# Scores of layer 0 in pairs, a padded router row, and gate and up products three experts ahead

## The reference

```
layer 0 attention: projection -> 8 attention heads (64 wide, rotary, causal)
                   + 4 retention heads (64 wide keys, 128 wide values, decay,
                     group norm, swish gate) -> output projection
layer 1 attention: projection -> 16 heads, dilated causal windows -> output projection
experts (both):    g = top1(x @ w_group + b_group)          # 4 groups
                   i = top2 of (x @ w_fine + b_fine) in g   # 8 experts a group
                   out[t] += gate * (silu(x @ w_gate[e]) * (x @ w_up[e])) @ w_down[e]
```

## Time and profile before

| | |
|---|---|
| median of 3 runs | 1133.7 us (1133.15 to 1136.21) |
| profiled execution | 1135.6 us, span 1133.7 us |
| TensorE busy | 861.8 us (76% of the span) |
| TensorE weight load busy | 547.3 us (48%) |
| VectorE, ScalarE, GpSimd busy | 383.3, 244.2, 37.8 us |
| DMA | 440.71 MB, mean 389 GB/s |
| mean granted TensorE clock | 0.883 |

### The profile page before, as it was taken

The page is one execution under the profiler, slowest core; times in us unless marked ns, Lnnn a source line. Parts: engine busy times, 40 slices in busy tenths (PEclk is TensorE's granted clock), DMA queues, the critical chain, the costliest instruction groups (busy, mean ns, idle before and its releaser), DMA issues.

```text
span 1133.7 us, 21763 instructions
## 1 busy us (share of the span) xinstructions
PE 861.8 (76%) x9154; PEld 547.3 (48%) x9154; DVE 383.3 (34%) x940; ACT 244.2 (22%) x624; POOL 37.8 (3%) x59
## 2 busy tenths in 40 slices
PE   8999979967675657576899999798566666666774
PEld 6876735534343434243478776455243434343432
DVE  6886523322120212121188763333121212121212
ACT  5565401100000100000165763111000000000012
POOL 0014000000000000000000220000000000000000
PEclk9998989988687878888999999899787879797887
DMA  9967889999999999999996577999999999999995
GB/s 344 277 288 298 366 331 412 430 427 428 431 427 428 430 428 428 429 428 428 415 386 276 213 309 287 419 427 429 428 428 429 427 430 428 427 430 428 428 428 217
DMA packets 54417, 440.71 MB, mean 389 GB/s; under 512 B 11873, under 2 KB 12385, under 8 KB 29538
## 3 DMA queue, kind: packets, MB, share of 16 engines
q1 hardware_dynamic: 54368, 440.07, 93.5%
q10 hardware_dynamic: 2, 0.00, 0.0%
HBM read 439.01 MB, written 1.05 MB: 388 GB/s over the span
## 4 chain that ended last, share of the span: by engine, by line
PE 43%; DMA 40%; SPq 5%; DVE 4%; another core or an unknown queue 3%; ACT 3%; issue 2%; POOL 0%; POOLq 0%; ACTq 0%; DVEq 0%
DMA ring<-in_w_expert_up 30%; PE bank L1039 13%; DMA ring<-in_w_expert_down 9%; PE bank L1060 5%; PE bank L933 3%; PE bank L935 3%; PE bank L934 3%; SPq L449 3%; PE bank L1073 3%; PE bank L1021 2%; PE bank L1121 1%; SPq L453 1%; PE bank L1123 1%; PE bank L1122 1%
## 5 line engine op out<-in xcount | busy, mean ns | idle before, releaser
L1039 PE MATMUL bank<-ring,scratch 128*32 128x256 f32 x4096 | 302.2, 460 | 177.8 <-DMA ring<-in_w_expert_up 176.4
L1039 PEld LDWEIGHTS bank<-ring,scratch 128*32 128x32 f32 x4096 | 156.5, 132 | 319.1 <-issue 208.5
L1488 DVE TENSOR_SCALAR scratch<-scratch 128x128 f32<-128x128 f32 x64 | 14.5, 227 | 634.3 <-ACT scratch L726 612.5
L725 ACT ACTIVATE scratch<-bank 128x128 f32<-128x128 f32 x64 | 17.7, 277 | 587.6 <-PE bank L1039 568.9
L1060 PE MATMUL bank<-ring,h 128*32 128x256 f32 x2048 | 127.2, 390 | 11.3 <-DMA ring<-in_w_expert_down 11.3
L1073 PE MATMUL bank<-h 32*128 32x256 f32 x1024 | 75.5, 407 | 37.2 <-ACT h L733 37.2
L1060 PEld LDWEIGHTS bank<-ring,h 128*32 128x32 f32 x2048 | 63.1, 111 | 55.8 <-issue 24.1
L1073 PEld LDWEIGHTS bank<-h 32*128 32x128 f32 x1024 | 50.9, 188 | 67.1 <-issue 67.0
L933 PE MATMUL bank<-split,h_high 128*128 128x512 f32 x192 | 77.6, 404 | 2.0 <-DVE split L1302 1.4
L934 PE MATMUL bank<-split,h_low 128*128 128x512 f32 x192 | 75.1, 391 | 0.0
L935 PE MATMUL bank<-split,h_high 128*128 128x512 f32 x192 | 75.1, 391 | 0.0
(11 more groups left out here) (166 smaller groups left out, 741.9 us busy)
## 6 DMA issues: line engine op xcount, KB each, us to landing
ring<-in_w_expert_gate SPq DMA_DIRECT2D x64, 2048.0 KB, 47.3
ring<-in_w_expert_up SPq DMA_DIRECT2D x64, 2048.0 KB, 48.8
ring<-in_w_expert_down SPq DMA_DIRECT2D x62, 2048.0 KB, 48.5
ring<-in_w_in_even SPq DMA_DIRECT2D x5, 2048.0 KB, 17.9
ring<-in_w_in_odd SPq DMA_DIRECT2D x5, 2048.0 KB, 20.5
ring<-in_w_out_even SPq DMA_DIRECT2D x2, 2048.0 KB, 8.3
ring<-in_w_expert_down SPq DMA_DIRECT2D x4, 1024.0 KB, 44.4
ring<-in_w_out_odd SPq DMA_DIRECT2D x2, 2048.0 KB, 12.9
```

The costliest lines, as they stand in the source:

```text
L1039: last = pe.matmul(psum[6][32 * j:32 * j + 32, 0:2 * P].rearrange("p (a s) -> p a s", a=2), xT[:, c, SLOTS * k:SLOTS * k + SLOTS], ring[:, ...
```

## The change

- In layer 0 the scores of two heads are issued together, each pair waiting for both maxima of the pair before. VectorE works by pairs too: two maxima, a step of the retention statistics, then the two reciprocals. The four retained products are split, two behind the first pair of scores and two behind the second. The power steps on GpSimd go ahead of head 4 in place of head 3, and the two gating products come after all heads.
- The router's logits become one row of 40 columns: 4 groups, 4 columns of padding (zero weight, bias of -3e38), 32 experts. VectorE makes it in one operation in place of two and masks in place. The filler between the two counting parts is one product of 512 columns and one of 128 in place of two of 512.
- Gate and up products run three experts ahead (`AHEAD` 3 in place of 2). The third product goes behind the start of the sums; SP reloads pairs 4, 5 and 6 before down 4; the gather of the next group comes one expert earlier. In a layer's last group the filler, or the spreading of the gain row, stays behind steps 0 and 1, while the last gate and up product now stands behind step 0.
- Some small tiles move. `SPLIT_FIRST` keeps the old value 2 where the projection of layer 1 used `AHEAD`.

```
+FINE_AT = 8
+ROUTES = FINE_AT + 32
...
-AHEAD = 2
+AHEAD = 3
+SPLIT_FIRST = 2
...
-        w_rt = sb("w_rt", [P, LAYERS, C, GROUPS + EXPERTS])
-        b_rt = sb("b_rt", [P, LAYERS, GROUPS + EXPERTS])
-        small = sb("small", [P, 320])
+        w_rt = sb("w_rt", [P, LAYERS, C, ROUTES])
+        b_rt = sb("b_rt", [P, LAYERS, ROUTES])
...
-        masked = scratch[:, 1536:1600].rearrange("p (t e) -> p t e", t=T)
-        chosen = scratch[:, 1600:1728].rearrange("p (t c e) -> p t c e", t=T, c=2)
-        lf = scratch[:, 1728:1792].rearrange("p (t e) -> p t e", t=T)
+        routes = scratch[:, 1536:1536 + T * ROUTES].rearrange("p (t e) -> p t e", t=T)
+        lg, lf = routes[:, :, 0:FINE_AT], routes[:, :, FINE_AT:ROUTES]
+        chosen = scratch[:, 1664:1792].rearrange("p (t c e) -> p t c e", t=T, c=2)
...
-                for e in range(EXPERTS - 8, EXPERTS - 6):
+                for e in range(EXPERTS - 2 * GE, EXPERTS - GE - AHEAD):
                     step(r * EXPERTS + e, e, e % GE)
 
             def load_across(l, r):
 
-                for k in range(6):
-                    e = r * EXPERTS + k - 6
-                    next_down(l, e, EXPERTS - AHEAD + k if k < AHEAD else k - AHEAD, (k + AHEAD) % GE)
+                for k in range(GE + AHEAD):
+                    e = r * EXPERTS + k - (GE + AHEAD)
+                    next_down(l, e, EXPERTS - AHEAD + k if k < AHEAD else k - AHEAD, (k - AHEAD) % GE)
...
-                for e in range(2):
+                for e in range(AHEAD):
...
-                next_down(l, more * EXPERTS + EXPERTS - 6, EXPERTS - 2, GE - 2)
+                for e in range(EXPERTS - GE - AHEAD, EXPERTS - GE - 1):
+                    next_down(l, more * EXPERTS + e, e + GE, e % GE)
...
-                    if l == 0 and m == 3:
+                    if l == 0 and m == 4:
...
-                    if l == 0 and m >= HEADS[0] - T:
-                        t = m - (HEADS[0] - T)
+                if l == 0:
+                    for t in range(T):
...
-                        parts(AHEAD if l else 1, 4)
+                        parts(SPLIT_FIRST if l else 1, 4)
...
-                    pe.wait_ge(s_out[l], m - 1 if l == 0 else m - 2)
+                    pe.wait_ge(s_out[l], m if l == 0 else m - 2)
                 elif l == 0:
-                    pe.wait_ge(ret_ready, RET - 1 + m)
-                heads = [(score_bank(l, n), slice(HEAD * (n % 2), HEAD * (n % 2) + HEAD))
-                         for n in ((m,) if l == 0 else (m, m + 1))]
+                    pe.wait_ge(ret_ready, RET)
+                heads = [(score_bank(l, n), slice(HEAD * (n % 2), HEAD * (n % 2) + HEAD)) for n in (m, m + 1)]
                 q, k = qT[:, m // 2, :], kT[:, m // 2, :]
                 for bank, rows in heads:
...
-                elif l == 0 or i % 2 == 0:
+                elif i % 2 == 0:
...
+                    if not after and k < 2:
+                        if l == LAYERS - 1:
+                            spread_gains(k)
+                        else:
+                            keep_warm(4, cst[:, 0:512], psum[5])
                     if k < GE - AHEAD:
-                        if not after and l == LAYERS - 1:
-                            spread_gains(k)
-                        elif not after:
-                            keep_warm(4, cst[:, 0:512], psum[5])
                         gate_up(l, r, g, k + AHEAD)
...
-                    last = pe.matmul(psum[4 + t][:, 0:36], hT(t, q)[:, c - 4 * q, :],
+                    last = pe.matmul(psum[4 + t][:, 0:ROUTES], hT(t, q)[:, c - 4 * q, :],
...
-                        for n in range(n_ret[l]):
+                    if l == 0 and m in (1, 3):
+                        for n in (m - 1, m):
...
-                keep_warm(2, cst[:, 0:512], psum[0])
+                keep_warm(1, cst[:, 0:512], psum[0])
+                keep_warm(1, cst[:, 0:128], psum[0])
...
+                for k in range(2, AHEAD):
+                    gate_up(l, 0, 0, k)
...
-                if m in (2, 3):
-                    t = m - 2
+                if m in (2, 4):
+                    t = m // 2 - 1
...
-                elif m in (6, 7):
...
+            def retention_norm(t):
+
+                if t == 0:
+                    dve.wait_ge(ret_pow, 6)
+                    dve.wait_ge(swished, T)
+                for n in range(RET):
+                    at = RET * t + n
+                    last = dve.tensor_scalar(o_ret[:, t, P * n:P * n + P], psum[6 + t][:, P * n:P * n + P],
+                                             rstat[:, t, n, 0:1], rrstd[:, at:at + 1], ALU.subtract, ALU.mult)
+                last.then_inc(ret_scaled, 1)
...
-                for dst, cols in ((lg[:, t, 0:GROUPS], slice(0, GROUPS)), (lf[:, t, :], slice(GROUPS, 36))):
-                    last = dve.scalar_tensor_tensor(out=dst, in0=bank[:, cols], scalar=rstd[:, t:t + 1],
-                                                    in1=bias[:, cols], op0=ALU.mult, op1=ALU.add)
-                link(last)
+                link(dve.scalar_tensor_tensor(out=routes[:, t, :], in0=bank[:, 0:ROUTES], scalar=rstd[:, t:t + 1],
+                                              in1=bias, op0=ALU.mult, op1=ALU.add))
...
+            dve.memset(w_rt[:, :, :, GROUPS:FINE_AT], 0.0)
+            norm_link(dve.memset(b_rt[:, :, GROUPS:FINE_AT], -FAR))
...
-                    if m < HEADS[l]:
+                    if l and m < HEADS[l]:
                         head_max(l, m)
+                    if l == 0 and m < HEADS[l] and m % 2 == 0:
+                        head_max(l, m)
+                        head_max(l, m + 1)
+                        retention_step(m, link)
+                        head_sum(l, m, link)
+                        if m == HEADS[l] - 2:
+                            retention_norm(0)
+                        head_sum(l, m + 1, link)
+                        if m == HEADS[l] - 2:
+                            retention_norm(1)
...
-                    if 0 < m <= HEADS[l]:
+                    if l and 0 < m <= HEADS[l]:
                         head_sum(l, m - 1, link)
-                    if l == 0 and m <= HEADS[l]:
-                        retention_step(m, link)
...
-                for k in range(AHEAD):
+                for k in range(2):
                     hidden(l, k, k, first=(k == 0))
                 dve.wait_ge(gate_steps, GATE_STEPS * (l + 1))
                 for k in range(AHEAD):
                     gate_slots(l, k, k)
+                for k in range(2, AHEAD):
+                    hidden(l, k, k)
```

More of the change, by code:

```diff
@@ L221, in build @@
         gains_rt = sb("gains_rt", [P, LAYERS, C])
[L222 to L224 removed]
+        w_rt = sb("w_rt", [P, LAYERS, C, ROUTES])
+        b_rt = sb("b_rt", [P, LAYERS, ROUTES])
+        small = sb("small", [P, 306])
         idx_u = sb("idx_u", [P, 2 * T, 8], U32)
@@ L313, in build @@
         bnst = small[:, 258:306].rearrange("p (a s) -> p a s", a=2 * RET)
-        expg = small[:, 306:314].rearrange("p (t e) -> p t e", t=T)
+        expg = small[:, 136:144].rearrange("p (t e) -> p t e", t=T)
         sq4 = small[:, 256:264].rearrange("p (t a) -> p t a", t=T)
-        half_exp = small[:, 314:316]
-        cnt = small[:, 316:318]
-        three_halves = small[:, 318:319]
+        half_exp = small[:, 144:146]
+        cnt = small[:, 146:148]
+        three_halves = small[:, 148:149]
         newton = small[:, 258:266]
-        posm = sb("posm", [P, T, 36])
-        gate = sb("gate", [P, T, 36])
+        posm = sb("posm", [P, T, EXPERTS])
+        gate = sb("gate", [P, T, EXPERTS])
         asg = sb("asg", [P, T, EXPERTS])
         gterm = sb("gterm", [P, T, 2, EXPERTS])
-        limhit = sb("limhit", [P, MAX_ROUNDS - 1])
+        limhit = small[:, 184:184 + MAX_ROUNDS - 1]
         x_loaded = sems("x_loaded", T)
@@ L556, in _ @@
                         for dst, src in ((w_rt[:, m, :, 0:GROUPS], w_group[m].rearrange("(c p) e -> p c e", c=C)),
-                                         (w_rt[:, m, :, GROUPS:], w_fine[m].rearrange("(c p) e -> p c e", c=C)),
+                                         (w_rt[:, m, :, FINE_AT:], w_fine[m].rearrange("(c p) e -> p c e", c=C)),
                                          (b_rt[:, m, 0:GROUPS], b_group[m].partition_broadcast(P)),
-                                         (b_rt[:, m, GROUPS:], b_fine[m].partition_broadcast(P))):
+                                         (b_rt[:, m, FINE_AT:], b_fine[m].partition_broadcast(P))):
                             sp.dma_start(dst, src).then_inc(router_loaded, 16)
@@ L886, in _ @@
                     act.wait_ge(gain_loaded[2 * l + 2], 16)
-                    split_chunks(l + 1, 0, 0, AHEAD)
+                    split_chunks(l + 1, 0, 0, SPLIT_FIRST)
                 act.wait_ge(scattered[l], (more + 1) * EXPERTS)
@@ L1392, in retention_step @@
                                           ALU.add).then_inc(ret_var, 1)
-                elif m in (6, 7):
-                    t = m - 6
-                    if t == 0:
```

(21 more changed lines are left out.)

4 lines of the change are left out of this document (1 added, 3 removed).

## The result

| | before | after |
|---|---|---|
| median | 1134.26 us (12 runs, 1132.34 to 1136.21) | 1137.28 us (12 runs, 1134.83 to 1139.19) |
| profiled execution, span | 1135.6, 1133.7 us | 1136.6, 1134.7 us |

The ratio is 1.0026, 95% interval 1.0019 to 1.0033: the change costs 3.0 us. I had forecast a gain of 0.6 and 1133.1 us; the median lies 0.1 us outside the range and in the other direction. The kernel before measured 1134.3 us here, 0.6 above the median that I forecast from, so 3.0 us is the number to explain.

What follows compares the result with a forecast made beforehand. The weight stream at 428 GB/s was taken to bound the expert stages, leaving the time to each layer's first product and the layer ends. Pairs -1.7, router -1.2 and -0.3, ends +2.0 and +0.6 gave -0.6: 1133.1 us, range 1129.2 to 1137.2.

Steps and rivals of the forecast that it cites:

- Three ahead, at the start of a stage: First products of a stage: product 2 ahead of down 0, stream never dry, down 0 1 to 2 us later; cost 0.
- Three ahead, at the end: Last group of a layer: filler or spreading now delays downs 30 and 31; loss 2.0 us layer 0, 0.6 layer 1.
- Rival (a): Layer ends: last downs bound by landing alone, filler hidden, so no cost; 1128.0 us, or 1130.5 breaking even; chance 0.16.
- Heads in pairs: Layer 0 attention heads: second early piece of the output projection starts sooner; gain 1.7 us, ends 0 and 2.4.
- Rival (b): Layer 0 heads: pairs gain nothing, GpSimd's power steps start later and the clock stays at half; 1134.8 us, chance 0.13.
- Router: Router of both layers: shorter filler and one logits operation fewer bring counting products sooner; gain 1.2 us layer 0, 0.3 layer 1.
- Rival (c): After the router's counting products: less filler, clock falls, 3.4 us lost per layer; 1136.5 us with one, 1139.9 both; chance 0.11.
- Sum: Whole kernel: - 1.7 - 1.2 + 2.0 - 0.3 + 0.6 = - 0.6 us, median 1133.1 us.

Runs made afterwards that it cites:

- the repetition: The changed kernel, nothing altered, profiled and measured a second time against the kernel before: 1137.8 us, ratio 1.0038 [1.0023, 1.0052].

## Why the prediction was wrong

**Three ahead, at the start of a stage: the step that failed.** It said cost 0, down 0 "may start 1 to 2 us later". Down product 0 ended 14.0 us later relative to the first reload (31.6 against 17.6), and it was the next thing SP waited for. I counted six units as a stream that "does not run dry" and never set their 29.4 us against the end of down product 0. The parts of the 14 us: product 2 ended 16.0 us after the first reload (158.93 - 142.89) where the turned gates of down 0 had started at 13.3 before (159.87 - 146.53), 2.7 us; the stall under the branch 6.2; the second stall 4.2; 0.9 is left, which is in down product 0's own records: they took 4.5 us without the stall, against 3.64 before, at the 1.2 GHz level in both. The 1 to 2 us of the prediction were the first part alone. The row was in the trace of before: a branch of 6.29 us that began at 150.7, under the start of the sums and a wait put down to VectorE. I read the wait's releaser and not what else lay under it. Shown by taking the branch away with its code (no stall, no hole), and by a late down product alone (a hole without the change); moving the product past the branch showed that any late release does it.

**Three ahead, at the end: right.** Forecast a loss of 2.0 and 0.6. The tail from the end of the stream to the last scatter grew by 2.2 us in layer 0 (7.6 against 5.4; 1.5 in the repetition) and 0.6 in layer 1 (5.3 against 4.7), with filler, down 30 and down 31 back to back. Rival (a), ends that cost nothing, is refuted by that chain.

**Heads in pairs: mechanism right, size a little high.** Forecast 1.7, about 1.1 by the medians, whose intervals overlap. The early piece came at 102.3 to 104.0 us in eleven of the twelve traces with the pairs (105.8 in the other), against 104.6 and 105.0 in the two without: the forecast of 102.9 lies within, on the early side. The half-clock stretch behind the heads lasted 3.4 us in six of the twelve and 6.8 in the other six. Rival (b), all 1.7 us lost, is not borne out.

**Router: 1.5 forecast, about 1.1 measured, and not for the reason given.** In layer 0 the counting products came behind VectorE as forecast in the first trace; in the repetition the filler ran at half clock, took 2.48 us and ended last. The way from the early piece to the first reload got 1.3 us shorter where the router ran at full clock. But it got as short with the long filler. As far as the one trace of before shows, what went was the half-clock stretch over the filler and not its columns, and in five traces a longer stretch came back and cost 0.4 us more than before.

**Rival (c)** had the right sign by the wrong mechanism: the half-clock stretch in the router does occur, at 1.7 us in place of the 3.4 that it priced, but in the kernel two ahead, which is 5 us quicker, as well as in the changed one.

**Sum.** -1.1 (pairs), -1.1 (router), +2.2 and +0.6 (ends), and the hole in layer 0, +2.0 against the stream of before (414.9) or +2.7 against 414.2: +2.6 to +3.3, against a measured +3.0. The first two terms are the uncertain ones. The traces add up by themselves, against the one of before: in the first trace of the changed kernel the first reload came 3.6 us earlier, stage 0 was 4.2 longer, the way to layer 1's first reload 0.5 shorter and stage 1 0.9 longer, which is the +1.0 us of its span; in the repetition -0.6, +3.2, -0.6 and +0.9, which is its +3.0. The forecast had the first reload 2.9 us earlier; it was so in one of the two.

The Trainium skill has a rule that I did not weigh: "Runtime: NRT & Kernel Launch", section "Instruction fetch mechanics", says that a taken branch to a target outside the sequencer's small window forces a DMA fetch before execution goes on, in blocks of 16 KiB. The trace agrees: 6.4 us for the branch, and three packets of 0.05 MB together on the instruction queue in 155 to 176 us. The packets' own times tie them to the stalls. One of 16 KB moved from 162.3 to 163.3 us and the branch ended at 164.8; the next moved from 168.7 to 169.7 and the second stall ended at 171.0. In all the traces here each of the 26 branches and each of the five second stalls ended 1.3 to 1.6 us behind such a packet. The packet itself took about 1 us, and it began only 3.3 to 4.3 us after the branch did: most of the stall lies ahead of it. That it starts late because the weights fill the rings is argued from their place, not shown; no run here emptied the rings around the branch.

## What to carry to other kernels

A cheap-looking instruction under a wait is only as cheap as its cover: before moving work into a wait, list everything on that engine's queue under it, branches included. When a queue's requests are issued in a fixed order, set the time of the next release against the units asked for: here six units last 29.4 us, and down product 0 ended 2 us after that, which the stream did not make good. The version to keep is this change with the run ahead left at two: 0.9988 and 0.9984 of the kernel before in two comparisons, intervals below 1 in both.

## What was not expected of the hardware

A conditional branch on TensorE over a long piece of code took 5.8 to 6.6 us in each of the 26 cases in these traces, while weights streamed at some 420 GB/s. The code behind it stalled once more, by 3.7 to 4.7 us and five records in, in five cases: all in layer 0, and all where work was ready right behind the branch. With a wait for VectorE or filler behind the branch, or in layer 1, it did not; what decides is open. And the same program has or hasn't a half-clock stretch of 6.8 us in its router from one execution to the next, worth 1.7 us.
